# DRAM layout of the delta operands: one record per chunk and head against channel and token tensors in the order of the scan

## The reference, cut to what matters

```
decay = exp(where(tril, g[..., :, None] - g[..., None, :], -inf))
attn = where(tril, einsum('bhncd,bhnsd->bhncs', q, k) * decay, 0.0)
k_tail = k * exp(g_last - g) ; q_head = q * exp(g)
def step(state, inp):
    v_new = u_i - wk_i @ state
    o_i = q_i @ state + attn_i @ v_new
    state = state * exp(gl_i) + einsum('bhcd,bhce->bhde', k_i, v_new)
    return state, o_i
```

## Time and profile before

| | us |
|---|---|
| runs shown: median of 3 (lowest to highest) | 4449.22 (4447.55 to 4461.03) |
| the profiled execution | 4440.76 |
| its span, first to last instruction | 4439.1 |
| PE busy | 3672.3 |
| DVE busy | 2147.5 |
| POOL busy | 786.9 |

### The profile page before, as it was taken

The page is one execution under the profiler, slowest core; times in us unless marked ns, Lnnn a source line. Parts: engine busy times, 40 slices in busy tenths (PEclk is TensorE's granted clock), DMA queues, the critical chain, the costliest instruction groups (busy, mean ns, idle before and its releaser), DMA issues. The chain is left out here.

```text
span 4439.1 us, 64109 instructions
## 1 busy us (share of the span) xinstructions
PE 3672.3 (83%) x28116; PEld 2864.8 (65%) x28116; DVE 2147.5 (48%) x2188; ACT 646.0 (15%) x1002; POOL 786.9 (18%) x818
## 2 busy tenths in 40 slices
PE   7499999999997988289999999976467636888793
PEld 1277777777886876168878888854345534677383
DVE  0457787753334542544453343346678834321633
ACT  0022222212000001110110000011133201222001
POOL 0001111111000000025005134000673775000000
PEclk9799999999998999589999999987689767988797
DMA  7355555555343432322233243334458598765222
GB/s 265 106 153 153 151 152 152 152 171 168 103 123 101 141 99 108 107 69 85 77 101 90 80 114 109 111 137 171 126 178 252 158 220 187 187 195 179 72 95 114
DMA packets 666347, 611.49 MB, mean 138 GB/s; under 512 B 150656, under 2 KB 567480, under 8 KB 657760
## 3 DMA queue, kind: packets, MB, share of 16 engines
q1 hardware_dynamic: 567808, 435.15, 34.3%
q0 software_dynamic: 21936, 95.56, 6.6%
q10 hardware_dynamic: 76336, 76.83, 5.3%
HBM read 471.67 MB, written 135.82 MB: 137 GB/s over the span
## 5 line engine op out<-in xcount | busy, mean ns | idle before, releaser
L361 PE MATMUL front_ps<-b_hT,front_wb 128*128 128x512 f32 x4224 | 979.1, 392 | 18.3 <-DVE front_wb L351 18.3
L1251 PE MATMUL in_ps<-b_hT,in_wb 128*128 128x512 f32 (+3 forms) x4992 | 956.4, 353 | 10.7 <-DVE in_wb L1238 10.7
L361 PEld LDWEIGHTS front_ps<-b_hT,front_wb 128*128 128x128 f32 x4224 | 789.7, 188 | 199.0 <-DVE front_wb L351 21.6
L1251 PEld LDWEIGHTS in_ps<-b_hT,in_wb 128*128 128x128 f32 (+1 forms) x4992 | 816.2, 188 | 157.5 <-issue 15.4
L1236 DVE CAST in_wb<-in_raw 128x2048 fp32r<-128x2048 f32 (+1 forms) x68 | 82.6, 1215 | 560.5 <-PE in_ps L1251 543.0
L349 DVE CAST front_wb<-front_raw 128x2048 fp32r<-128x2048 f32 x88 | 108.0, 1228 | 433.8 <-PE front_ps L361 425.1
L755 POOL DMA_DIRECT2D front_mwb<-in_w_ada x128 | 101.7, 798 | 803.6 <-PE front_mps L765 800.9
L351 DVE TENSOR_TENSOR front_wb<-front_raw,front_wb 128x2048 fp32r<-128x2048 f32 x88 | 201.8, 2293 | 3.0
L1003 PE MATMUL merge_ps<-merge_pair,merge_wb 128*128 128x512 f32 x768 | 176.5, 392 | 22.3 <-DVEq L1021 22.3
L1086 PE MATMUL wout_ps<-wout_wb,wout_pair 128*128 128x512 f32 x768 | 176.6, 392 | 15.2 <-DVEq L1107 14.5
L1086 PE MATMUL wo_ps<-wo_wb,wo_pair 128*128 128x512 f32 x768 | 176.8, 392 | 12.9 <-DVEq L1107 12.2
(11 more groups left out here) (420 smaller groups left out, 4715.4 us busy)
## 6 DMA issues: line engine op xcount, KB each, us to landing
front_raw<-in_w_in SPq DMA_DIRECT2D x88, 1024.0 KB, 6.7
in_raw<-in_w_in SPq DMA_DIRECT2D x67, 1024.0 KB, 5.6
front_mwb<-in_w_ada POOLq DMA_DIRECT2D x128, 512.0 KB, 5.1
r_scr<-rprep_ob ACTq DMA_DIRECT2D x16, 2694.0 KB, 13.0
scan_rops<-r_scr SPq DMA_DIRECT2D x24, 1796.0 KB, 11.1
mod_wb<-in_w_ada SPq DMA_DIRECT2D x8, 4096.0 KB, 12.7
g_scr<-gprep_ob SPq DMA_DIRECT2D x8, 3474.0 KB, 11.2
wo_raw<-in_w_o SPq DMA_DIRECT2D x16, 1024.0 KB, 5.0
```

The costliest lines, as they stand in the source:

```text
L361: last = self.nc.tensor.matmul(self.ps[:, n % 2, :], self.wb[:, n % 2, x, kt, :], self.hT[:, y, kt, :], start=kt == term == 0, stop=kt == ...
L1251: last = self.nc.tensor.matmul(self.ps[0:width, n % 3, first:end], self.wb[:, n % 2, x, kt, 0:width], self.hT[:, y, kt, first:end], start= ...
```

## The change

`g_scr` is replaced by two tensors whose order is that of the scan's loads. `g_chan` is (chunk, direction, partition, head, 129), and `g_tok` (chunk, partition, head, 321). A head's operands are now stored by three DMAs in place of one: `ob`'s channel columns of direction 0, those of direction 1, and the token columns. So the semaphore `stored` counts 80 per head in place of 48. The loads of the scan stay four per step, with the same bytes, but each partition's data are contiguous in DRAM: 4128 bytes for `chan`, 10272 bytes for `tok`. Nothing else changes; `ob`, `chan` and `tok` have the same shapes in SBUF, and no computation differs.

```
@@ DeltaPrep.heads, DeltaPrep.exponentials
-            dve.wait_ge(self.stored[u], 48 * (i // 2))
+            dve.wait_ge(self.stored[u], 80 * (i // 2))
...
-            act_e.wait_ge(self.stored[u], 48 * (i // 2))
+            act_e.wait_ge(self.stored[u], 80 * (i // 2))
@@ DeltaPrep.store
-        sp.dma_start(self.g_scr[:, i:i + 1].rearrange("c h p x -> p (c h) x"), self.ob[:, u]).then_inc(self.stored[u], 16)
+        for d in range(2):
+            sp.dma_start(self.g_chan[:, d, :, i, :].rearrange("c p x -> p c x"),
+                         self.ob[:, u, :, G_CH * d:G_CH * (d + 1)]).then_inc(self.stored[u], 16)
+        sp.dma_start(self.g_tok[:, :, i, :].rearrange("c p x -> p c x"), self.ob[:, u, :, 2 * G_CH:G_COLS]).then_inc(self.stored[u], 16)
@@ DeltaPrep.finish
-            sp.wait_ge(self.stored[u], 48 * GH // 2)
+            sp.wait_ge(self.stored[u], 80 * GH // 2)
@@ DeltaScan.load
-            rows = self.g_scr[STEPS[k][d]].rearrange("h p x -> p h x")
-            sp.dma_start(self.chan[:, u, d], rows[:, :, G_CH * d:G_CH * (d + 1)]).then_inc(self.loaded[u], 16)
-            sp.dma_start(self.tok[r, u], rows[r, :, 2 * G_CH:G_COLS]).then_inc(self.loaded[u], 16)
+            sp.dma_start(self.chan[:, u, d], self.g_chan[STEPS[k][d], d]).then_inc(self.loaded[u], 16)
+            sp.dma_start(self.tok[r, u], self.g_tok[STEPS[k][d], r]).then_inc(self.loaded[u], 16)
@@ program
-    g_scr = dram("g_scr", (NCH, GH, P, G_COLS))
+    g_chan = dram("g_chan", (NCH, 2, P, GH, G_CH))
+    g_tok = dram("g_tok", (NCH, P, GH, G_TOK))
```

More of the change, by code:

```diff
@@ L1736, with __init__ @@
     ROWS = InverseNorms.ROWS
-    def __init__(self, nc, st, k, p2, norms, gT, g_scr, systems):
-        self.nc, self.k, self.p2, self.norms, self.gT, self.g_scr, self.systems = nc, k, p2, norms, gT, g_scr, systems
+    def __init__(self, nc, st, k, p2, norms, gT, g_chan, g_tok, systems):
+        self.nc, self.k, self.p2, self.norms, self.gT, self.systems = nc, k, p2, norms, gT, systems
+        self.g_chan, self.g_tok = g_chan, g_tok
         self.x = st.sb("x", [P, 3, 3, TA])
@@ L1959, in finish, with delta_prep @@
         for u in range(2):
-            sp.wait_ge(self.stored[u], 48 * GH // 2)
-def delta_prep(nc, k, p2, norms, gT, g_scr, systems):
+            sp.wait_ge(self.stored[u], 80 * GH // 2)
+def delta_prep(nc, k, p2, norms, gT, g_chan, g_tok, systems):
     with Stage(nc, "gprep") as st:
-        m = DeltaPrep(nc, st, k, p2, norms, gT, g_scr, systems)
+        m = DeltaPrep(nc, st, k, p2, norms, gT, g_chan, g_tok, systems)
         with nc.Block() as block:
@@ L2488, with __init__ @@
     H = GH // 2
-    def __init__(self, nc, st, g_scr, systems, slots):
-        self.nc, self.g_scr, self.systems, self.slots = nc, g_scr, systems, slots
+    def __init__(self, nc, st, g_chan, g_tok, systems, slots):
+        self.nc, self.g_chan, self.g_tok, self.systems, self.slots = nc, g_chan, g_tok, systems, slots
         self.chan = st.sb("gchan", [P, 2, 2, GH, G_CH])
@@ L3043, with scans @@
 LAG = 8
-def scans(nc, k, p2, gain, vectors, bonus, g_scr, r_scr, v_scr, systems, slots, late, yT):
+def scans(nc, k, p2, gain, vectors, bonus, g_chan, g_tok, r_scr, v_scr, systems, slots, late, yT):
     with Stage(nc, "scan") as st:
-        g = DeltaScan(nc, st, g_scr, systems, slots)
+        g = DeltaScan(nc, st, g_chan, g_tok, systems, slots)
         r = RwkvScan(nc, st, r_scr, v_scr, systems, yT[:, GH:2 * GH])
@@ L3234, in program @@
                 second(nc, k, a, hT, gT, p2, norms)
-            delta_prep(nc, k, p2, norms, gT, g_scr, systems)
+            delta_prep(nc, k, p2, norms, gT, g_chan, g_tok, systems)
         rwkv_prep(nc, k, p2, norms, a["rwkv_w_up_2"][0], a["rwkv_a_up_2"][0], a["rwkv_vectors"], r_scr, v_scr, bonus, systems)
@@ L3243, in program @@
                 slots = [gT[:, 2 * c:2 * c + 2, :].rearrange("p a n -> p (a n)") for c in range(T // C // 2)] + [late[:, c] for c in range(T // C // 2)]
-                scans(nc, k, p2, a["gdn_norm_g_2"][0].unsqueeze(1), a["rwkv_out_vectors"], bonus, g_scr, r_scr, v_scr, systems, slots, late, y2T)
+                scans(nc, k, p2, a["gdn_norm_g_2"][0].unsqueeze(1), a["rwkv_out_vectors"], bonus, g_chan, g_tok, r_scr, v_scr, systems, slots, late, y2T)
             y = s1.sb("y", [P, TT, D])
```

## The result

The changed kernel takes 4467.09 us (median of 8 runs, 4458.39 to 4475.54) beside 4453.95 (8 runs of the kernel before). The ratio is 1.0028, 95% interval [1.0015, 1.0042]: 12.5 us slower by the ratio, 13.1 by the medians. Run once more on another occasion it was 1.0034 [1.0022, 1.0046]. The forecast was no change with 2.3 us less, in a range that ended at 4460. It is slower by just under the 13.3 us (0.3%) that had been named as the bound, and by two causes that stood among the rivals, each in part.

The account below looks back on a forecast made before the run. Compute paces delta_prep except its bare last store; POOL's chain ends the scans' first stretch. Stores +1.2 and POOL's moves -3.5 give -2.3 us on 4440.8: 4438.5, or 4446.9 on the runs' scale; range 4434 to 4460.

Parts of the forecast that it names:

- the 13.3 us (0.3%): Whole kernel: about what a measurement can tell from no change; same had chance 0.80, faster 0.10, slower 0.10.
- The price of the stores: End of delta_prep: three short-piece stores take 10.4 us per head in place of 9.2, so +1.2 us.
- rival 3: End of delta_prep: small stores run at 180 GB/s, last two heads lose 16.8 us, total 4466; chance 0.10.
- What hides them: delta_prep: seven of eight heads hide the longer stores behind SP's 119.4 us of waiting; only the last costs +1.2 us.
- its sign of 25: After delta_prep's last store: a stretch with only DMA running above 25 us would show the slow small stores.
- its term for the head before: delta_prep: the head before the last holds the engines 19.8 + 1.9 - 15.5 = 6.2 us more.
- The loads: Scans: `chan` rises from 323 to 395 GB/s, `tok` stays at 192; 0.6 us less per step, worth nothing themselves.
- What POOL gains: Scans: faster delta loads shorten POOL's second move by 1.1 us and third by 2.4, together -3.5 us.
- rival 2: Scans: long load rows stand in POOL's way, each move 12.1 us, +8.2 us, with stores 4458.6; chance 0.14.
- its +5.2 for the last move: Scans: POOL's fourth move, a store of 6.9 us, grows to 12.1 us beside long load rows.

Follow-up runs that it names:

- the holds: Kernels after and before, with SP delaying step 4's delta loads until POOL's second load landed: 1.0026 and 1.0000; before with step 8's loads delayed too: 1.0020.
- e2: Changed kernel with both scan loads cut into 516 and 1284 byte pieces by an SBUF gap; 1.0008 [0.9999, 1.0018] to the kernel before.
- e3: Changed kernel in which SP delays the loads of delta step 4 until POOL's second load has landed; 1.0026 [1.0013, 1.0038] to the kernel before.

## Why the prediction was wrong

**The price of the stores: wrong by a factor.** The step was "4.9 + 5.5 = 10.4 us, so +1.2 us per head". It took 516-byte stores at the 323 GB/s of 516-byte reads, and 1284-byte ones at 360 near the 376 of the 1796-byte stores. Head 5 and its systems took 22.5 us to move in place of 12.5, so some 10 us more a head and not 1.2, and over 8 us of it they ran at 137 GB/s. A read rate was no neighbour for a store, and the 256-byte pieces at 271 GB/s all start at a multiple of 256 bytes. The change's pieces start at multiples of 516 or 1284. That a start off a boundary costs a short store has no term in the sum. Starts come up once, under rival 3, where unaligned 1796-byte pieces at 376 GB/s stand against a loss; they are long, as are the 2316 bytes of before, and short pieces are where it counts.

**What hides them: wrong for the last head.** "Seven of the eight heads hide it" and "SP's 119.4 us of waiting covers them" were checked for the average. The gap of 15.5 us before the last head is the case that counts. Head 6's transfers were not through when it came, and SP had been blocked by their issue: 1.3 us in the start and, by the estimate above, some 5 of the 7.9 in the bare stretch. This is the mechanism of rival 3, which named the slow head and what the head before leaves over, took 180 GB/s, 16.8 us for the two, and got a chance of 0.10. Its rate was near: head 5 ran at 172 GB/s over 23 us. But the last head, with no compute beside it, moved at 236. The loss was 9.2 us, below the 13.3 that the rival needed, and the bare stretch 21.7 us, below its sign of 25. The 1.9 us in its term for the head before have no working in the prediction.

**The loads: right, and worth nothing, as said.** `tok` stayed near 192 GB/s and `chan` went to about 400, 395 foretold. PE's wait before the first RWKV step grew from 21.67 to 37.81 us. The end of the first stretch was POOL's chain, which the holds show.

**What POOL gains: wrong sign.** The step was "-1.1" and "-2.4" for the second and third move. They grew by 2.2 and 3.2 us. It reasoned from the bytes that share the engines. But the third move was already slow beside small pieces, and rows that are long and slow at once made it slower. That long rows lengthen POOL's moves is rival 2. It foretold 12.1 us for each move, which is +3.0 us for the three visible ones together; +5.2 was measured. The second, 11.4 and 12.0 measured, is hardly above the kernels with short rows. The third, 17.7 and 16.8, is the one that long rows made slower, and there the rival had 2.4 us less than before. Of its +5.2 for the last move nothing came (6.8 us after, 6.9 before): SP's loads of that iteration were issued by 3746.8, 24 us ahead of it.

Stores 9.2 and first stretch 4.7 us make 13.9, against 12.5 [6.7, 18.7] by the ratio. That the two add up so well is in part luck, as e2 and e3 show parts and times that agree less. So the mechanisms of two rivals, with 0.24 between them, acted together, each with about half of its price, and the range counted them one at a time: 4460 held rival 2 alone. Their sum, 4449 + 16.8 + 8.2 = 4474, was never formed. Chance had a share as well: the forecast stood on three runs with a median of 4449.22, where the eight runs beside the result have 4453.95. Moved up by that, the range would have ended at 4464.7, still below 4467.09.

## What to carry to other kernels

Moving a rearrangement from the loads to the stores pays only where the loads end something and the stores don't; look for the last store before a barrier, and for the shortest gap ahead of it, not the average one. Where store pieces must be short, give them a pitch of a multiple of 64 bytes; here it took back 5.5 of the 7.9 us in the bare stretch. And before a transfer is made of long rows, ask whose DMA on another queue shares the engines with it: here a chain of 1.5 MB moves lost more than the faster loads gained.

## What the runs showed of the hardware

- Stores to DRAM in 516 and 1284 byte pieces with starts off multiples of 64 bytes: 137 GB/s over 8 us beside compute, where 2316-byte pieces ran at 357 in the same window. The head whose pieces start at multiples of 32 bytes ran at 228, against 131 to 142 for the six behind it. In head 5 the rate is near 290 GB/s for the first microsecond, and then falls. With starts at multiples of 64 bytes the bare stretch was 16.2 us in place of 20.9 to 21.9.
- Loads into 64 of the 128 partitions ran at 181 to 194 GB/s whatever the length of their pieces (256, 1284 or 10272 bytes), in windows of 2.5 to 4.5 us.
- Beside rows of 10272 bytes in SP's queue a 1.5 MB load of POOL took 16.8 to 17.8 us (three kernels), beside token pieces of 1284 bytes 13.0 to 15.5 (eight kernels).
- Issuing a DMA can hold SP for long when much is queued: 11.28 us for two stores of 192 KB behind short pieces, 6.38 behind the old store.
